# Seven half-size block products instead of eight for an MLP's up product, and the up product run a unit ahead of all of the down product

## The reference, cut to what matters

```
h2 = rms_norm(x, norm_mlp)                     # x: 512 x 1024
x  = x + square(relu(h2 @ w_ff1)) @ w_ff2      # w_ff1: 1024 x 4096, w_ff2: 4096 x 1024
return rms_norm(x, norm_final)
```

## Time and profile before

| | us |
|---|---|
| median of 3 runs (1690.90 to 1691.43) | 1690.91 |
| the profiled execution, its own time | 1689.05 |
| its span, first to last instruction | 1687.4 |
| PE busy | 1672.0 (99%) |
| VectorE busy | 896.4 (53%) |
| ScalarE busy | 618.6 (37%) |
| GpSimd busy | 112.8 (7%) |

### The profile page before, as it was taken

The page is one execution under the profiler, slowest core; times in us unless marked ns, Lnnn a source line. Parts: engine busy times, 40 slices in busy tenths (PEclk is TensorE's granted clock), DMA queues, the critical chain, the costliest instruction groups (busy, mean ns, idle before and its releaser), DMA issues.

```text
span 1687.4 us, 23046 instructions
## 1 busy us (share of the span) xinstructions
PE 1672.0 (99%) x9378; PEld 1217.1 (72%) x9378; DVE 896.4 (53%) x1217; ACT 618.6 (37%) x744; POOL 112.8 (7%) x168
## 2 busy tenths in 40 slices
PE   9999999999999999999999999999999999999998
PEld 7888888865454535454588877788888888888886
DVE  6425438452343334324668755567675544773487
ACT  6334433321111101111366633344642245652565
POOL 4000000000000000000011012210000001100100
PEclk9999999999999999999999999999999999999999
DMA  7332222948999999999541332124352358756974
GB/s 274 100 99 75 75 75 101 354 189 342 429 428 428 428 429 429 428 429 428 204 153 53 100 100 75 51 76 132 107 188 100 107 181 195 157 149 221 200 157 128
DMA packets 90703, 353.29 MB, mean 209 GB/s; under 512 B 7856, under 2 KB 7872, under 8 KB 78208
## 3 DMA queue, kind: packets, MB, share of 16 engines
q1 hardware_dynamic: 78288, 325.95, 50.4%
q0 software_dynamic: 12336, 26.23, 7.8%
HBM read 345.87 MB, written 6.29 MB: 209 GB/s over the span
## 4 chain that ended last, share of the span: by engine, by line
PE 97%; DMA 1%; DVE 1%; ACT 0%; issue 0%; POOL 0%; DVEq 0%; POOLq 0%; ACTq 0%
PE bank L2764 51%; PE bank L3117 12%; PE bank L3522 9%; PE bank L3130 7%; PE bank L3025 4%; PE bank L3065 3%; PE bank L3297 2%; PE bank L2789 2%; PE bank L2810 1%; DMA ring<-in_w 1%; PE bank L3327 1%; PE bank L3350 1%; PE bank L3397 1%; PE bank L3222 1%; PE bank L3430 0%; PE bank L3436 0%
## 5 line engine op out<-in xcount | busy, mean ns | idle before, releaser
L2764 PE MATMUL bank<-act_hi,w_hi 128*128 128x512 f32 x992 | 390.0, 393 | 0.0
L2764 PE MATMUL bank<-act_hi,w_lo 128*128 128x512 f32 x992 | 386.2, 389 | 0.0
L2764 PE MATMUL bank<-act_lo,w_hi 128*128 128x512 f32 x992 | 386.2, 389 | 0.0
L1754 DVE TENSOR_TENSOR w_lo<-w_stage,w_hi 128x2048 fp32r<-128x2048 f32 x79 | 181.1, 2293 | 208.9 <-ACT w_hi L1044 208.8
L1044 ACT ACTIVATE w_hi<-w_stage 128x2048 fp32r<-128x2048 f32 x79 | 151.4, 1917 | 242.0 <-PE bank L2764 223.7
L3117 PE MATMUL bank<-ring,xgT 128*64 128x512 f32 x992 | 216.1, 592 | 1.8 <-ACT xgT L1266 1.4
L2764 PEld LDWEIGHTS bank<-act_hi,w_hi 128*128 128x128 f32 x992 | 186.2, 188 | 40.8 <-issue 2.9
L2764 PEld LDWEIGHTS bank<-act_hi,w_lo 128*128 128x128 f32 x992 | 186.2, 188 | 39.1
L2764 PEld LDWEIGHTS bank<-act_lo,w_hi 128*128 128x128 f32 x992 | 186.3, 188 | 37.7
L3117 PEld LDWEIGHTS bank<-ring,xgT 128*64 128x64 f32 x992 | 71.0, 137 | 143.0 <-issue 139.5
L3130 PE MATMUL bank<-ring,gatedT 128*64 128x512 f32 x512 | 113.4, 595 | 3.1 <-DMA ring<-in_w 2.3
(11 more groups left out here) (490 smaller groups left out, 2366.6 us busy)
## 6 DMA issues: line engine op xcount, KB each, us to landing
ring<-in_w SPq DMA_DIRECT2D x94, 2048.0 KB, 16.8
w_stage<-in_w_in SPq DMA_DIRECT2D x42, 1024.0 KB, 5.1
w_stage<-in_w_ff SPq DMA_DIRECT2D x24, 1024.0 KB, 5.6
b_sum<-in_w_ff POOLq DMA_DIRECT2D x12, 1024.0 KB, 12.7
w_stage<-in_w_out SPq DMA_DIRECT2D x8, 1024.0 KB, 5.0
b_one<-in_w_ff SPq DMA_DIRECT2D x6, 1024.0 KB, 7.7
branch_gates<-gate_out POOLq DMA_DIRECT2D x16, 256.0 KB, 2.5
w_stage<-in_w_proj_gla SPq DMA_DIRECT2D x4, 1024.0 KB, 9.9
```

Of the source, the lines that this page charges most:

```text
L1754: dve.tensor_tensor(w_lo[s][:, 0:ktiles, :], w_stage[s][:, 0:ktiles, :], w_hi[s][:, 0:ktiles, :].bitcast(F32), ALU.subtract).then_inc(w_lo ...
L2764: ins = pe.matmul(banks[j][:, :], left, right, start=(kc == 0 and k == 0 and n_pass == 0), stop=(kc == g.chunks - 1 and k == g.ktiles - 1 ...
```

## The change

The eight units are no longer tied to the halves. Unit 0 is computed as before. Units 1 to 7 (`BLOCKED` = 7) are each computed by the same seven-product scheme as the down product: left operands are 512 x 256 blocks of the weights and sums of them (`w_add`, W1 to W4, on VectorE), right operands are 512 x 256 blocks of the turned rows and sums of them (`t_add`, T1 to T4, made once). One product is 2 x 4 x 3 = 24 matmuls of 256 columns. The weight splits go through three slots (`slot_hi`, `slot_lo`) of half the size, in turn. Four output blocks of a unit come out of the banks by three copies on ScalarE, three additions on VectorE, and relu and square on ScalarE. Only after unit 7 come the down products of half 0 and half 1, without an up product between them. The turned rows are copied from their bank once (`raw_T`), and both halves are made from the copy.

The diff, cut to its core. SP's list:

```diff
-            for h, (up, down) in enumerate(g_ff):
...
+            for u in range(1, BLOCKED + 1):
+                if u == 1:
+                    sp.wait_ge(w_lo_done, split_count(g_up.chunk0))
+                else:
+                    sp.wait_ge(hid_summed, w_summed(u - 1, W3))
+                load_rows(w_stage[0][:, :, :], 0, 512 * u, 512, w_loaded[0])
+                if u == 1:
+                    sp.wait_ge(w_lo_done, split_count(g_up.chunk0 + 1))
+                else:
+                    sp.wait_ge(hid_summed, w_summed(u - 1, W4))
+                load_rows(w12, 1, 512 * u, 256, w_loaded[1])
+                if u > 1:
+                    sp.wait_ge(w_lo_done, blk_split(u - 1, 6))
+                load_rows(w22, 1, 512 * u + 256, 256, far_loaded)
+                if u == 2:
+                    sp.wait_ge(n_sd, rows_count(5, NT - 1))
+                    for kc in range(2):
+                        sp.dma_start(b_sum[0][kc][:, :, :], weight_block(0, 0, 1, kc)).then_inc(b_sum_in[kc], 16)
+            sp.wait_ge(hid_summed, w_summed(BLOCKED, W3))
+            sp.dma_start(w_stage[0][:, :, :], weight_block(0, 0, 0, 0)).then_inc(w_loaded[0], 16)
+            sp.wait_ge(w_lo_done, blk_split(BLOCKED, 5))
+            sp.wait_ge(pe_tiles, products_done(BLOCKED, 3))
+            sp.dma_start(b_one[1][:, :, :], weight_block(0, 0, 1, 0)).then_inc(b_one_in[1], 16)
+            sp.dma_start(b_far[:, :, :], weight_block(0, 0, 1, 1)).then_inc(b_one_in[0], 16)
+            sp.wait_ge(w_lo_done, blk_split(BLOCKED, 6))
+            sp.dma_start(w_stage[1][:, :, :], weight_block(0, 0, 0, 1)).then_inc(w_loaded[1], 16)
+            for h in range(HALVES):
                 for kc in range(2):
                     sp.wait_ge(w_lo_done, step(h, kc))
                     sp.dma_start(w_stage[kc][:, :, :], weight_block(h, 1, 0, kc)).then_inc(w_loaded[kc], 16)
+                more = h + 1 < HALVES
+                if more:
+                    sp.wait_ge(w_lo_done, step(h, 6))
+                    sp.dma_start(w_stage[0][:, :, :], weight_block(h + 1, 0, 0, 0)).then_inc(w_loaded[0], 16)
                 sp.wait_ge(part_low, V_PARTS + PARTS * h + 3)
                 sp.wait_ge(hid_summed, summed_in(h) + S4)
                 sp.dma_start(b_one[0][:, :, :], weight_block(h, 1, 1, 0)).then_inc(b_one_in[0], 16)
+                if more:
+                    sp.wait_ge(w_lo_done, step(h, 7))
+                    sp.dma_start(w_stage[1][:, :, :], weight_block(h + 1, 0, 0, 1)).then_inc(w_loaded[1], 16)
                 sp.wait_ge(w_lo_done, step(h, 8))
                 sp.dma_start(b_one[1][:, :, :], weight_block(h, 1, 1, 1)).then_inc(b_one_in[1], 16)
+                if more:
+                    sp.wait_ge(part_low, V_PARTS + PARTS * h + 5)
+                    for kc in range(2):
+                        sp.dma_start(b_sum[1][kc][:, :, :], weight_block(h + 1, 0, 1, kc)).then_inc(b_sum_in[kc], 16)
+                    sp.wait_ge(w_lo_done, step(h, 10))
+                    sp.dma_start(b_far[:, :, :], weight_block(h + 1, 0, 1, 1)).then_inc(b_one_in[0], 16)
```

ScalarE's list:

```diff
+            split_hi(g_up.chunk0 + 1, 1)
+            t_high(T2)
+            t_high(T3)
+            for t in range(NT):
+                mlp_squares(t)
...
+            slot_high(1, 0)
+            slot_high(1, 1)
+            for j in range(4):
...
+                act.activation(relu_t[j % 2][:, :], gb[j][:, :], ACT.Relu).then_inc(out_act, 1)
...
+            for u in range(1, BLOCKED + 1):
+                slot_high(u, 2)
+                if u == 1:
+                    t_high(T1)
+                copy_first(u)
+                slot_high(u, 3)
...
+                slot_high(u, 4)
...
+                copy_both(u)
...
+                slot_high(u, 5)
+                copy_fifth(u)
+                slot_high(u, 6)
+                relu_sum(u, ADD_11, blk_first)
+                if u < BLOCKED:
+                    slot_high(u + 1, 0)
+                else:
+                    part_split_hi(0, 0)
+                square(u, 0, 0, blk_first)
+                if u < BLOCKED:
+                    slot_high(u + 1, 1)
+                else:
+                    step_split_hi(0, 0)
+                relu_sum(u, ADD_22, blk_fifth)
+                square(u, 1, 1, blk_fifth)
+                if u in (3, 4):
+                    negate_sums(0, u - 3)
+            step_split_hi(0, 1)
+            relu_sum(BLOCKED, ADD_12, blk_both)
+            square(BLOCKED, 0, 1, blk_both)
+            relu_last(BLOCKED)
+            square(BLOCKED, 1, 0, blk_last)
+            part_split_hi(0, 1)
+            for h in range(HALVES):
                 step_split_hi(h, 2)
+                for kc, block in enumerate((b_one[1], b_far)):
+                    act.wait_ge(b_one_in[1 - kc], loaded(h, "one", 1))
+                    negate(block, block)
                 for n in range(PARTS - 2):
                     step_split_hi(h, 2 * n + 3)
                     part_split_hi(h, n + 2)
...
                     step_split_hi(h, 2 * n + 4)
...
+                    elif h + 1 < HALVES:
+                        negate_sums(h + 1, n - 3)
```

VectorE's list:

```diff
+            for u in range(1, BLOCKED + 1):
+                first, second, third = blk_banks(u)
+                w_add(u, W1)
+                w_add(u, W2)
+                slot_low(u, 2)
...
+                slot_low(u, 3)
+                w_add(u, W3)
+                w_add(u, W4)
+                slot_low(u, 4)
...
+                blk_add(u, ADD_11, 1, CP_FIRST, blk_first, second)
+                slot_low(u, 5)
+                slot_low(u, 6)
+                if u == BLOCKED:
+                    part_split_lo(0, 0)
+                blk_add(u, ADD_22, 4, CP_FIFTH, blk_fifth, first)
+                if u < BLOCKED:
+                    slot_low(u + 1, 0)
+                else:
+                    step_split_lo(0, 0)
+                blk_add(u, ADD_12, 5, CP_BOTH, blk_both, third)
+                if u < BLOCKED:
+                    slot_low(u + 1, 1)
+            step_split_lo(0, 1)
+            part_split_lo(0, 1)
```

More of the change, by code:

```diff
@@ L126, in two_blocks @@
     FH = FF // HALVES
[L127 to L132, removed]
+    g_up = Gemm(g_out2, 1, 2, "act")
+    BLOCKED = FF // 512 - 1
+    g_blk = Gemm(g_up, BLOCKED, PARTS, "act", tiles=3)
+    sums_added = g_blk.out["dve"]
+    g_blk.out["dve"] += 3 * BLOCKED
+    g_down = []
+    for h in range(HALVES):
+        g_down.append(Gemm(g_down[-1] if h else g_blk, 2, PARTS, "dve", tiles=PARTS))
     gates_dram = nc.dram_tensor("branch_gates", [2 * KT, P, T], F32).ap()
@@ L373, in two_blocks @@
[L373 to L377, removed]
+        part_hi = [at(f"part_hi{s}", page, [P, 8, 256], F32R) for s, page in enumerate((F + 32, 13))]
+        part_lo = [at(f"part_lo{s}", page, [P, 8, 256], F32R) for s, page in enumerate((F + 36, 17))]
@@ new lines, in two_blocks @@
+        b_one = [at(f"b_one{s}", page, [P, 4, 512]) for s, page in enumerate((25, 21))]
+        s_two = at("s_two", 25, [P, 8, 256])
+        b_sum = [[at(f"b_sum{h}{s}", page + 4 * s, [P, 4, 512]) for s in range(2)] for h, page in enumerate((F + 40, F + 0))]
+        down_hi = [at(f"down_hi{s}", page, [P, 4, 512], F32R) for s, page in enumerate((45, 41))]
+        down_lo = [at(f"down_lo{s}", page, [P, 4, 512], F32R) for s, page in enumerate((37, 49))]
+        relu_t = [at(f"relu_t{s}", F + 52 + s, [P, T]) for s in range(2)]
@@ new lines, in two_blocks @@
+        slot_page = (41, 45, 37)
+        slot_hi = [at(f"slot_hi{s}", page, [P, 4, 256], F32R) for s, page in enumerate(slot_page)]
+        slot_lo = [at(f"slot_lo{s}", page + 2, [P, 4, 256], F32R) for s, page in enumerate(slot_page)]
+        w11, w21 = w_stage[0][:, :, 0:256], w_stage[0][:, :, 256:512]
+        w12, w22 = w_stage[1][:, :, 0:256], w_stage[1][:, :, 256:512]
+        w_sum = [at(f"w_sum{s}", 8 + 2 * s, [P, 4, 256]) for s in range(2)]
+        raw_T = at("raw_T", F + 12, [P, KT, T])
@@ new lines, in slot_low, with blk_add @@
+            def slot_low(u, n):
+                s = product(u, n) % 3
+                dve.wait_ge(w_hi_done, blk_split(u, n))
+                source = (w11, w12, w_sum[1][:, :, :], w_sum[0][:, :, :], w_sum[0][:, :, :], w_sum[1][:, :, :], w22)[n]
+                rest(slot_lo[s][:, :, :], source, slot_hi[s][:, :, :]).then_inc(w_lo_done, 1)
+            def blk_add(u, n, last_product, copied, t, bank):
+                dve.wait_ge(pe_tiles, products_done(u, last_product))
+                dve.wait_ge(out_act, blk_copied(u, copied))
+                dve.tensor_tensor(t[:, :], bank[:, :], t[:, :], ALU.add).then_inc(out_dve, 1)
@@ L3525, in part_passes @@
                 ins.then_inc(pe_tiles, 2)
-            for h, (up, down) in enumerate(g_ff):
-                if h == 0:
-                    first_up(up)
-                else:
-                    gemm(up, fm=True, ready=lambda kc, j, h=h: kc == 0 and pe.wait_ge(out_dve, added(h - 1, *last_add[j])))
+            first_up(g_up)
```

(4 more changed lines are left out.)

447 lines of the change are left out of this document (296 added, 151 removed).

## The result

| | before | after |
|---|---|---|
| median (lowest to highest), us | 1690.91 (1690.76 to 1691.43) | 1708.03 (1706.98 to 1709.85) |
| the profiled execution, its own time | 1689.05 | 1709.85 |
| its span | 1687.4 | 1708.1 |

The changed kernel takes 1.0102 times as long, 95% interval 1.0084 to 1.0119, 4 runs each. 1705 was predicted, with 1688 to 1716 as the range. In every profile the span ends with the same list of rows and a store.

A forecast was written before the change was run, and what follows sets the result against it. PE was taken to bound the kernel, so any wait of it costs in full. Waits of 25.7 us less 11.4 of matmul time add 14.3 to 1689.05, giving 1703.3; with 1.86 for the median, 1705, range 1688 to 1716.

The forecast's parts named there:

- matmul time: Units 1 to 7: 20.16 us each at 0.1200 a matmul instead of 21.8, 11.4 us less together.
- (a): Entry: copy, splits and row squares on ScalarE delay units 0 and 1, 2.4 us.
- (b): Unit 6: three adds in a row delay the loads of w_stage[0], w12 and w22, 6.0 us.
- (c): Unit 7 into the down product: waits at product 6, step 1 and step 2, 4.4 us.
- (d): Half 0, step 6: add 4, queued behind add 3, lands late, 1.5 us.
- (e): Half 0, step 11: its split stands behind a negation waiting for the late load of b_sum[1][0], 6.1 us.
- (f): Half 1, S' its step 0: late second load of w_stage[0], 2.6, and late add 4, 2.7; 5.3 us.
- Rival 4: Matmuls of 256 columns cost 0.1133 us each: 1697 us, chance 4%.
- rival 5: ScalarE's and VectorE's lists bound every unit, each losing 1.2 us more: 1713 us, chance 8%.
- Rivals 1 to 3: Plain loads undelayed, 1686.3, 15%; no wait at half 0's step 11, 1699, 15%; neither that nor unit 6's, 1693, 8%.
- upper bounds: Largest waits allowed: entry 3, unit 6 8, into down product 5.5, step 6 2.3, step 11 8, half 1 4 twice.

The follow-up runs named there:

- few_adds_all: Changed kernel with each of the 20 adding transfers cut to 128 of 2048 elements a partition: 1687.09 us, ratio 0.9974 to the kernel before.
- experiment 11: no_swap with the four row squares moved from ahead of slot_high(1, 0) to the ends of units 1 and 2, b_sum[0] transfers one unit later: 1696.05 us.
- few_adds_early: Changed kernel with only the four adding transfers in units 4 to 6 cut to 128 of 2048 elements a partition: 1701.98 us.
- spread_adds: Changed kernel with b_sum negations ending units 2 and 3, and adds 2 of half 0 held to one adding transfer per unit: 1701.03 us.
- sp_order: Changed kernel with SP issuing b_sum[1][0] straight behind b_one[0], ahead of b_one[1] and both w_stage loads for half 1: 1706.44 us.
- Experiments 6 to 10: Changed kernel with adding transfers and loads reordered, singly or in combinations, nothing left out: 1712.59, 1706.44, 1697.24, 1697.56 and 1697.19 us.
- all_five: Changed kernel with order_entry, spread_adds, sp_order, add 4 ahead of add 3, and half 1's second add 2 held for w_stage loads: 1697.24 us.
- no_swap: all_five without the swap of adds 3 and 4: 1697.56 us, ratio 1.0037 to the kernel before.
- order_entry: Changed kernel with unit 7's ADD_22 ahead of the part's low, and w_stage[1]'s load ahead of b_one[1] and b_far: 1705.01 us.

## Why the prediction was right, and where it wasn't

The forecast, its side and most of its places were right. Point by point, in us; the last column is the part of the slow matmuls that only covered a wait, as other kernels' traces show it:

| step of the prediction | predicted | waits in the trace | slow matmuls | of these, over a wait |
|---|---|---|---|---|
| matmul time | -11.4 | -11.4 | | |
| (a) entry | 2.4 | 2.3 | | |
| (b) unit 6 | 6.0 | 6.0 | 2.75 | 1.9 |
| (c) into the down product | 4.4 | 3.4 | 1.75 | 1.2 |
| (d) add 4 in half 0 | 1.5 | 0.9 | | |
| (e) step 11 of half 0 | 6.1 | 6.75 | 2.8 | 0 |
| (f) half 1 | 5.3 | 3.0 | | |
| sum | 14.3 | 11.0 | 7.3 | 3.1 |

11.0 and 7.3 make 18.3, which agrees with the 18.5 us by which the stretch of the MLP grew. At full clock the waits would have been 11.0 + 3.1 = 14.1, so the slow matmuls themselves cost 4.2.

How near the number came is in part luck. Counted with what was covered, (b) was 1.9 too low and (f) 2.3 too high, so the sum of the waits comes out at 14.1 against 14.3. And the prediction added 1.86 us for the median, because the profiled execution of the kernel before lay so far below its median; the changed kernel's profiled execution was 1.8 above its median instead. The medians are 3 us from the forecast, the profiled execution 6.55 from its 1703.3.

- **Matmul time.** Units 2 to 5 run at exactly 0.1200 us a matmul (27 products in 77.76 us) without a gap. Rival 4 is excluded, and so is rival 5: in few_adds_all seven units pass without a wait except the ones at the entry and at the end. Rivals 1 to 3 fall with the waits of unit 6 and of step 11.
- **(a)** as predicted, and shown to be ScalarE's list by experiment 11.
- **(b)** Mechanism right, size low: 6.0 of waits and 1.9 that half clock covered. The load of `w_stage[0]` was issued at 1468.62, 7.2 after unit 5's start as laid out, but took 13.4 us and landed at 20.6 instead of 19.5. So the first wait is 2.87 instead of 1.6; the other two, 3.12 and 1.9, are near the 3.3 and 1.8 of the working. The full working gave 6.7; I took 6 in case packets of half the length take half the time (the last section).
- **(c)** 1.2, 1.8 and 1.4 were predicted, and waits of 1.37 and 2.07 measured. The third seems missing in the changed kernel, since step 1 runs at a clock of 0.76 there and covers it; in few_adds_early, few_adds_all, spread_adds and sp_order, where the clock holds, it is 1.2.
- **(d)** right in kind, 0.9 against 1.5.
- **(e)** right in place, cause and size (6.75 against 6.1). The load was issued at 1579.86 and took 17.46 us. From step 0 (1532.12) it landed at 65.2, not at 61.5, and step 11 was due at 64.6, not at 61.4: the working in (d) and (e) leaves out the 3.2 us of waits that (c) itself puts behind step 0. It left them out on both sides, so the wait came out right all the same.
- **(f)** too high: both of its waits are there, 1.3 and 1.7 against 2.6 and 2.7. The second load of `w_stage[0]` was issued 0.9 before S' (1622.57), as laid out, but landed at S' + 7.7 instead of 9.2, beside an add that landed at S' + 5.4. Why add 4 costs 1 us less than laid out is not isolated; in the ledger (e) and (f) trade against each other.
- **The range.** The prediction says that 1688 to 1716 leaves out a sum of upper bounds. It doesn't: they add up to 34.8 us, and 1690.9 + 34.8 - 11.4 is 1714.
- **The term that is missing** is the clock. Every wait was priced at its own length. Behind some of them PE's matmuls run at half clock, which cost 4.2 us. With the 2.1 us ahead of the MLP that is most of the 6.55 us between the sum (1703.3) and the profiled execution (1709.85). The profiled execution has the lowest granted clock of the four, so the others probably lost less by it; their half clock wasn't traced.
- **A thing that the prediction had right by its sums but not in words:** it treated (e) and (f) as two late loads. Experiments 6 to 10 point to one cause, DMA engines that are full from 1550 us on. My first expectations for sp_order and all_five, built on single waits, were 5 to 8 and 9 to 12 us too low.

What stays open: which part of the 11 to 13 us would go if blocks for half 1 could be loaded during the up product. `b_sum[1]` lies on the first pages of `hidden`, so it wasn't tried. Open too is whether an order without the added wait of no_swap would do better.

## What to carry to other kernels

When a stage is taken out between two others, add up what its time was hiding: transfers that were spread over 87 us of matmuls now have to fit beside another stage's. Make that sum per resource (here DMA engine time by kind of transfer, over the whole stretch) before pricing single waits. Where it came out near the stretch's length or above, as here in the down product, new orders moved the wait and didn't remove it, and only fewer transfers helped; where the loads have time to spare, full engines cost nothing. Price a wait of some us on TensorE with the half clock that may follow, but only where the next operands are ready in time.

## What the hardware showed that I had not expected

- **The clock after a wait.** In the MLP of the changed kernel PE's granted clock fell only in or behind waits. Behind the waits of 2.87 and 3.12 us in unit 6, 24 matmuls of 256 columns took 5.29 us at 0.50, 0.220 each instead of 0.120. Behind the 6.75 us before step 11, twelve of the 24 matmuls of 512 columns started 0.427 after the one before, the level of 1.2 GHz; the row is 8.26 long instead of 5.44. It isn't the same in every run: the same wait of 2 us before step 1 was followed by a clock of 0.76 in the changed kernel and of 1.00 in sp_order, and the same product 1 of unit 6 ran at 0.50 in the changed kernel and at 1.00 in order_entry. Behind each of the waits of 3.5 to 11 us before a step, one or two in every kernel that has the loss of the down product, it came, and cost 1.5 to 2.8 us. The Trainium skill (TensorE: Matmul & The Clock Gate, What's actually happening) says that this clock is gated by how busy the engine was lately and knows a half and a full rate; the two prices per matmul, 1.8 and 1.9 times those at full clock, agree with it.
- **Half the bytes, as many packets.** A load of 512 KB in rows of 1 KB, alone, lands 3.6 us after issue, against 5.5 for 1024 KB. Beside an add that saving shrinks. From 1481 to 1485 us of the changed kernel, when the first short load and an add were under way, 298 packets of the load queue passed against 300 of the adds, with 0.31 against 0.61 MB: one for one, as the earlier trace rows show it for whole rows. The load of `w12` landed 6.0 us after the 1024 KB ahead of it in its queue, 18.3 after its own issue. The row of a load alone, and the two queues from 1481 to 1485 us (packets, MB, share):

```profile
w_stage<-in_w_ff SPq DMA_DIRECT2D x1, 512.0 KB, 3.6
```
```profile
q0 software_dynamic: 300, 0.61, 82.5%
q1 hardware_dynamic: 298, 0.31, 27.9%
```
